# Feed-forward product on the raw stream, with each token's factor put on by GpSimd afterwards

## The chip, the core and the metric

One core of one Trainium2 chip. The metric is the device time of one execution in microseconds (us), the median of several executions. Five engines work side by side, each through its own queue in order, and meet at semaphores: TensorE (PE) multiplies matrices, VectorE (DVE) and GpSimd (POOL) do elementwise work, ScalarE (ACT) copies and applies functions, SyncE (SP) starts transfers.

## The reference, cut to what matters

Two blocks follow each other. The part that the change touches is the feed-forward layer of the first:

```python
h = rmsnorm(x, norm_ffn_g[l])          # x * rsqrt(mean(x*x) + eps) * g, per token
g = dwconv(jnp.einsum("bsd,df->bsf", h, w_gate[l]), conv_ffn_w[l])   # 3 taps over tokens
v = jnp.einsum("bsd,df->bsf", h, w_up[l])
x = x + jnp.einsum("bsf,fd->bsd", jax.nn.silu(g) * v, w_down[l])
```

There are 1024 tokens, 1024 channels, 2816 feed-forward channels. All is float32. The norm's factor `rsqrt(...)` is one number for each token.

## The kernel before

The stream x lies in SBUF as `stream` (`X`), 8 tiles of 128 channels by 1024 tokens. Every product is made of three: a value is split into a high part (rounded by a copy) and a low part (the value minus its high part), for the input (`norm_hi`, `norm_lo`, in code `HH`, `HL`) and for the weights (`w_hi`, `w_lo`), and high*high, low*high and high*low are added in PSUM. Weights come in slabs of 128x1024: SP loads `w_raw` (two buffers), ACT copies the high part (L1078), POOL subtracts for the low part (L429).

The order of the work on each engine is written out by hand; semaphores (`wait_ge`) join the queues. PSUM has 8 banks. Products go round the banks 0 to 3, banks 4 and 5 carry the norm's sums and factors, banks 6 and 7 hold intermediate pieces of the norm and the feed-forward result (`ACC`).

Around the change the program runs like this. The mixer's output product is four "down jobs" of 16 tiles, each tile 6 matmuls for 128 channels by 512 tokens (a half). DVE adds each tile to the stream (`add_out`, L1723), and PE may be four tiles ahead of it, since it writes bank t mod 4 only when the addition that read it is done. During the last down job the feed-forward norm begins: ACT squares each finished stream tile (`square`, L1096), POOL adds the squares up (`sums`, L464, 14 additions into `temp2`), PE sums over channels (`stat`, L644), ACT takes the root (`mean_root`, L1109), DVE the reciprocal (`rstd`, L1534), and PE spreads the factor over a bank (`spread`, L651). The first half's `stat` stands ahead of tile 12 of the down job and its `spread` ahead of tile 13; the second half's stand in the next product, ahead of k=4 and k=5. Numbers m run over 16 pieces: half m // 8, channel tile m % 8.

With the factor there, DVE makes each piece of the normalized stream, x times weight times factor (`scaled`, L1547), ACT copies its high part (`hi`, L1116), and DVE (`low`, L1558) or, for three pieces, POOL (`piece_low`, L448) subtracts. `apply_early` puts the first pieces behind additions 12 to 15, `apply` does the rest. The first feed-forward product, `gated_pair` (L697 to L699), takes the pieces as they are ready.

The feed-forward layer has 22 channel tiles f. Each takes a pair of slabs (gate and up), four product tiles of 24 matmuls. ACT reads a gate tile to `temp0` and an up tile to `temp1` (`ffn_tile`, L1146) in the order gate half 0, up half 0, gate half 1, up half 1, then copies the high parts of two coming weight slabs. DVE applies the three taps to `temp0` after the third read (`ffn_conv`, L1792, L1795, L1798), ACT the silu (L1277), DVE multiplies by `temp1` (L1804), ACT and DVE split the result (L1280, L1808). After each two f a down job of 16 tiles follows on PE, which DVE adds to the stream (`add_down`, L1604), behind the multiplication in DVE's queue. DVE also does six long reductions for the second block's modulation (`ada_products`, L1819) in each turn. A loop runs ten turns; POOL does nothing in it but the low parts of six slabs a turn. The last f has its halves in another order, gate first.

## Time and profile before

| | us |
|---|---|
| median of 3 runs | 2075.82 |
| lowest, highest | 2075.29, 2077.02 |
| the profiled execution, its time | 2077.7 |
| its span in the profile | 2076.0 |
| TensorE busy | 2052.3 (99%) |
| VectorE, ScalarE, GpSimd busy | 1207.4, 669.7, 786.1 |

The span is the time from the first to the last instruction; the execution's own time is 1.7 us more. The granted TensorE clock is 0.996 of full over the execution (2.4 GHz is full). An engine's idle time matters only where another engine waits for it, so the views of waits and of the chain that ended last are read before the busy shares. A matmul's duration in the rows is longer than the distance to the next: matmuls overlap, and the distance is what counts.

### The profile page before, as it was taken

The numbers are of one execution on the slowest core, as the hardware profiler recorded it, in microseconds if no ns is written. First come the engines' busy times: TensorE is split into PE (matmuls) and PEld (weight loads), VectorE is DVE, ScalarE is ACT, GpSimd is POOL, SyncE is SP. The second block draws the span as 40 slices with busy tenths as digits, with TensorE's granted clock in tenths as the row PEclk, the third lists the DMA queues.
The fourth block names the chain that finished last, engine by engine and source line by source line (L and its number), as shares of the span: only waits on it lengthen the run. The fifth ranks groups of instructions, "written<-read, shape, count | busy, mean of one in ns | idle before, by whom it ended". The sixth has DMA issues, their size and how long they took to land.

```text
span 2076.0 us, 24666 instructions
## 1 busy us (share of the span) xinstructions
PE 2052.3 (99%) x9284; PEld 1681.1 (81%) x9284; DVE 1207.4 (58%) x1674; ACT 669.7 (32%) x1147; POOL 786.1 (38%) x471
## 2 busy tenths in 40 slices
PE   9999999999999999999999999999999999999998
PEld 7888788888888888888878888888888878777886
DVE  7999476555644555455566454354464480597565
ACT  6323345221122221222254122122122271698112
POOL 4678826222221222222276132122132272465623
PEclk9999999999999999999999999999999999999998
DMA  4131112322123222232112021121121111010202
GB/s 166 62 112 45 37 51 91 122 101 94 67 110 113 101 73 88 101 121 102 41 39 64 31 71 41 31 71 40 41 61 41 41 42 60 20 43 21 72 11 81
DMA packets 44748, 141.24 MB, mean 68 GB/s; under 512 B 5616, under 2 KB 9856, under 8 KB 44672
## 3 DMA queue, kind: packets, MB, share of 16 engines
q1 hardware_dynamic: 31632, 100.68, 15.1%
q10 hardware_dynamic: 13040, 39.54, 5.1%
q8 instruction: 50, 0.82, 0.2%
q14 instruction: 26, 0.21, 0.0%
HBM read 135.98 MB, written 7.36 MB: 69 GB/s over the span
## 4 chain that ended last, share of the span: by engine, by line
PE 81%; POOL 9%; ACT 5%; DVE 4%; issue 2%; DMA 0%; POOLq 0%; ACTq 0%; SPq 0%; DVEq 0%
PE psum L630 25%; PE psum L632 24%; PE psum L631 24%; POOL temp L464 2%; POOL w_lo L429 2%; POOL temp L489 1%; ACT probs L1470 1%; POOL temp L522 1%; DVE psum L1547 1%; DVE norm_lo L1560 1%; PE psum L972 1%; PE psum L997 1%; PE psum L754 1%; PE psum L756 1%; PE psum L755 1%
## 5 line engine op out<-in xcount | busy, mean ns | idle before, releaser
L429 POOL TENSOR_TENSOR w_lo<-w_raw,w_hi 128x1024 fp32r<-128x1024 f32 x174 | 441.0, 2550 | 975.2 <-ACT w_hi L1078 969.4
L630 PE MATMUL psum<-norm_hi,w_hi 128*128 128x512 f32 x1632 | 636.3, 390 | 1.2 <-ACT temp L1146 1.2
L632 PE MATMUL psum<-norm_hi,w_lo 128*128 128x512 f32 x1632 | 635.0, 389 | 0.0
L631 PE MATMUL psum<-norm_lo,w_hi 128*128 128x512 f32 x1632 | 634.9, 389 | 0.0
L630 PEld LDWEIGHTS psum<-norm_hi,w_hi 128*128 128x128 f32 x1632 | 306.3, 188 | 65.6 <-issue 1.8
L632 PEld LDWEIGHTS psum<-norm_hi,w_lo 128*128 128x128 f32 x1632 | 306.3, 188 | 63.7
L631 PEld LDWEIGHTS psum<-norm_lo,w_hi 128*128 128x128 f32 x1632 | 306.4, 188 | 63.5 <-issue 0.2
L1146 ACT ACTIVATE temp<-psum 128x512 f32<-128x512 f32 x160 | 93.2, 598 | 397.5 <-PE psum L632 371.7
L1606 DVE SCALAR_TENSOR_TENSOR stream<-psum,mods,stream 128x512 f32<-128x512 f32 x160 | 119.7, 750 | 172.1 <-PE psum L632 172.1
L1078 ACT CAST w_hi<-w_raw 128x1024 fp32r<-128x1024 f32 x158 | 159.2, 1046 | 143.0 <-PE psum L632 79.6
L1604 DVE TENSOR_TENSOR stream<-psum,stream 128x512 f32<-128x512 f32 x176 | 118.7, 689 | 83.7 <-PE psum L632 83.5
L1692 DVE SCALAR_TENSOR_TENSOR psum<-glu,vec,psum 128x1024 f32<-128x1024 f32 x116 | 149.6, 1290 | 4.1
L630 PE MATMUL psum<-ffn_y_hi,w_hi 128*128 128x512 f32 x352 | 138.1, 392 | 0.0
L632 PE MATMUL psum<-ffn_y_hi,w_lo 128*128 128x512 f32 x352 | 137.1, 389 | 0.0
L631 PE MATMUL psum<-ffn_y_lo,w_hi 128*128 128x512 f32 x352 | 137.0, 389 | 0.0
L1819 DVE CUSTOM_DVE_ANT_0 ada_raw<-ada_raw,c_act 128x1024 f32<-128x1024 f32 x64 | 117.2, 1889 | 0.0
L1898 DVE TENSOR_TENSOR temp<-temp 128x1024 f32<-128x1024 f32 x40 | 77.4, 1935 | 52.3 <-ACT temp L1146 50.4
L1792 DVE TENSOR_SCALAR psum<-temp,vec 128x1024 f32<-128x1024 f32 x22 | 28.3, 1289 | 134.9 <-ACT temp L1146 134.6
L464 POOL TENSOR_TENSOR temp<-temp 128x512 f32<-128x512 f32 x54 | 70.1, 1298 | 95.4 <-ACT temp L1096 66.6
L630 PE MATMUL psum<-pool_y_hi,w_hi 128*128 128x512 f32 x256 | 99.8, 390 | 0.0
L632 PE MATMUL psum<-pool_y_hi,w_lo 128*128 128x512 f32 x256 | 99.6, 389 | 0.0
L631 PE MATMUL psum<-pool_y_lo,w_hi 128*128 128x512 f32 x256 | 99.6, 389 | 0.0
(218 smaller groups left out, 2968.8 us busy)
## 6 DMA issues: line engine op xcount, KB each, us to landing
w_raw<-in_slabs SPq DMA_DIRECT2D x175, 512.0 KB, 3.5
ada_raw<-in_ada ACTq DMA_DIRECT2D x10, 3072.0 KB, 12.2
stream<-in_x SPq DMA_DIRECT2D x8, 512.0 KB, 9.3
out<-stream SPq DMA_DIRECT2D x8, 512.0 KB, 2.8
skew_scratch<-row_scratch ACTq DMA_DIRECT2D x1, 3072.0 KB, 16.4
ada_raw<-in_ada ACTq DMA_DIRECT2D x1, 2048.0 KB, 7.8
bias<-skew_scratch ACTq DMA_DIRECT2D x4, 512.0 KB, 3.9
c_act<-in_c ACTq DMA_DIRECT2D x1, 512.0 KB, 9.7
```

Of the source, the lines that this page charges most:

```text
L429: nc.gpsimd.tensor_tensor(WL[place][:, :], RAW[at % 2][:, :], WH[place][:, :].bitcast(f32), ALU.subtract).then_inc(slab_ready, 1)
L464: nc.gpsimd.tensor_tensor(dst, squares(n, m - 1) if k == 1 else dst, squares(n, m), ALU.add).then_inc(sum_done, 1)
L630: nc.tensor.matmul(dst, wh, xh, start=n == 0, stop=False)
L631: nc.tensor.matmul(dst, wh, xl, start=False, stop=False)
L632: last = nc.tensor.matmul(dst, wl, xh, start=False, stop=n == len(terms) - 1)
L1078: nc.scalar.copy(WH[place][:, :], RAW[at % 2][:, :]).then_inc(w_hi_done, 1)
L1146: nc.scalar.activation(dst, bank[b], func, scale=scale).then_inc(act_read, 1)
L1604: ins = nc.vector.tensor_tensor(part, src, part, ALU.add)
L1606: ins = nc.vector.scalar_tensor_tensor(part, src, mods[:, gate + e:gate + e + 1], part, ALU.mult, ALU.add)
L1692: step(nc.vector.scalar_tensor_tensor(ACC, window, w, ACC, ALU.mult, ALU.add))
L1819: ins = nc.vector.tensor_tensor_reduce(out=ADA[:, n, :], in0=ADA[:, n, :], in1=c_act[:, :], scale=1.0, scalar=0.0, op0=ALU.mult, op1=ALU.a ...
L1898: step(nc.vector.tensor_tensor(body(T[dst]), body(T[src]), T[src][:, 16 - width:16 - width + S], ALU.add))
```

## The change

The first feed-forward product no longer takes the normalized stream but the stream times the norm's weight, without the token's factor. Each piece is split behind its addition in the last down job: ACT makes the high part in one instruction with the weight as scale, ahead of the square of the same piece, and DVE the low part from the stream, the weight and the high part, behind the next addition. The factor is computed as before; ACT copies it from banks 4 and 5 to `temp2`, where it stays for the whole layer. POOL multiplies it onto each half tile that ACT has read to `temp0` or `temp1`, and DVE's taps and multiplication wait for POOL (`f_scaled`) where they waited for ACT (`act_read`). The three pieces that POOL subtracted for this norm go.

```diff
+            gp.wait_ge(rstd_kept, 4)
+            def ffn_scale(f, order):
+                for n, (T_n, half) in enumerate(order):
+                    gp.wait_ge(act_read, 40 + 4 * f + n + 1)
+                    y = body(T[T_n], half)
+                    nc.gpsimd.tensor_tensor(y, y, body(T[2], half), ALU.mult).then_inc(f_scaled, 1)
+            ffn_scale(0, crossed)
             with gp.Fori(0, FFN_LOOPS) as i:
                 for n in range(FFN_SLAB + 6, FFN_SLAB + 12):
                     lower(n + 6 * i, n, SLAB_PLACE[n])
+                    if n in (FFN_SLAB + 7, FFN_SLAB + 9):
+                        ffn_scale(2 * i + (n - FFN_SLAB - 5) // 2, crossed)
...
-            norm_after_down(FFN, 48, ffn_slabs)
+            for m in range(16):
+                half, k = divmod(m, 8)
+                act.wait_ge(dve_read, 48 + m + 1)
+                nc.scalar.activation(HH[:, k, hs(half)], X[:, k, hs(half)], ACT.Identity, bias=zero[:, :],
+                                     scale=v("ffn_g", k)).then_inc(hi_done, 1)
+                square(FFN, m)
+                if m == STAT_AT[FFN] - 2:
+                    mean_root(FFN, 0)
+            mean_root(FFN, 1)
+            for half in range(2):
+                act.wait_ge(spread_done, spreads(FFN, half))
+                nc.scalar.copy(body(T[2], half), bank[4 + half]).then_inc(rstd_kept, 1)
+            weight_his(32, 34)
...
-            add_out(3, lambda m: apply_early(FFN, m))
-            apply(FFN, 16 - STAT_AT[FFN])
+            def ffn_plain_low(m):
+                half, k = divmod(m, 8)
+                dve.wait_ge(hi_done, m + 1)
+                nc.vector.scalar_tensor_tensor(HL[:, k, hs(half)], X[:, k, hs(half)], v("ffn_g", k),
+                                               HH[:, k, hs(half)].bitcast(f32), ALU.mult, ALU.subtract
+                                               ).then_inc(lo_done, 1)
+            def behind_last(m):
+                if m:
+                    ffn_plain_low(m - 1)
+                if m == STAT_AT[FFN] - 1:
+                    rstd(FFN, 0)
+            add_out(3, behind_last)
+            ffn_plain_low(15)
+            rstd(FFN, 1)
...
-                dve.wait_ge(act_read, a + (2 if last else 3))
+                dve.wait_ge(f_scaled, 4 * f + (2 if last else 3))
...
-                dve.wait_ge(act_read, a + 4)
+                dve.wait_ge(f_scaled, 4 * f + 4)
```

On DVE, at the end of the last down job (additions L1723, reciprocal L1534, the norm's pieces L1547 and L1558), the queue before reads:

```order
L1723 TENSOR_TENSOR stream<-psum,stream 128x512 x25
L1534 RECIPROCAL stat_column<-stat_column 128x4
L1723 TENSOR_TENSOR stream<-psum,stream 128x512
L1547 SCALAR_TENSOR_TENSOR psum<-stream,vec,psum 128x512
L1723 TENSOR_TENSOR stream<-psum,stream 128x512
L1547 SCALAR_TENSOR_TENSOR psum<-stream,vec,psum 128x512
L1558 TENSOR_TENSOR norm_lo<-psum,norm_hi 128x512
```

The same place on DVE after the change (L1738 is the addition, L1801 the new low part, L1549 the reciprocal):

```order
L1738 TENSOR_TENSOR stream<-psum,stream 128x512
L1801 SCALAR_TENSOR_TENSOR norm_lo<-stream,vec,norm_hi 128x512
L1738 TENSOR_TENSOR stream<-psum,stream 128x512
L1801 SCALAR_TENSOR_TENSOR norm_lo<-stream,vec,norm_hi 128x512
L1549 RECIPROCAL stat_column<-stat_column 128x4
L1738 TENSOR_TENSOR stream<-psum,stream 128x512
L1801 SCALAR_TENSOR_TENSOR norm_lo<-stream,vec,norm_hi 128x512
```

Between the additions there was nothing up to the reciprocal; now a low part with both inputs in SBUF stands behind each addition but the first, eleven of them ahead of the reciprocal.

On POOL, the queue from the sums of squares (L463) over the first channel tile to the first half of the loop, after the change (L428 is a slab's low part, L557 the new multiplication):

```order
L463 TENSOR_TENSOR temp<-temp 128x512 x14
L428 TENSOR_TENSOR w_lo<-w_raw,w_hi 128x1024 x4
L557 TENSOR_TENSOR temp<-temp 128x512 x4
L561 UNCONDITIONAL_BRANCH
L561 ISA
L428 TENSOR_TENSOR w_lo<-w_raw,w_hi 128x1024
L427 REGISTER_ALU
L428 TENSOR_TENSOR w_lo<-w_raw,w_hi 128x1024
L555 ISA
L557 TENSOR_TENSOR temp<-temp 128x512
L555 REGISTER_ALU
L557 TENSOR_TENSOR temp<-temp 128x512
```

Each turn of POOL's loop had six slab parts; now it has two, four multiplications, two, four multiplications and two.

## Rows read from the trace of the kernel before

**Rows 1.** The page: the span, and the busy time of each engine.

```profile
span 2076.0 us, 24666 instructions
...
PE 2052.3 (99%) x9284; PEld 1681.1 (81%) x9284; DVE 1207.4 (58%) x1674; ACT 669.7 (32%) x1147; POOL 786.1 (38%) x471
```

**Rows 2.** Waits, 300 to 356 us: waiter, releaser, us in all, times, longest.

```profile
PEld psum L697 <- DVE norm_lo L1558: 1.0, 3, 0.6
PEld psum L651 <- DVE stat_column L1534: 0.6, 1, 0.6
```

**Rows 3.** Waits of PEld (PE's weight loads), whole span.

```profile
PEld psum L630 <- DVE stream L1604: 3.7, 9, 0.4
```

**Rows 4.** Timeline of DVE, 286 to 385 us: start, us, line, what, idle before.

```profile
307.70 0.69 DVE L1723 TENSOR_TENSOR stream<-psum,stream 128x512 f32<-128x512 f32 x1 [1.12 <-PE psum L632]
...
322.21 0.69 DVE L1723 TENSOR_TENSOR stream<-psum,stream 128x512 f32<-128x512 f32 x1 [0.67 <-PE psum L632]
324.40 0.18 DVE L1534 RECIPROCAL stat_column<-stat_column 128x4 f32<-128x4 f32 x1 [1.50 <-ACT stat_column L1109]
324.51 0.69 DVE L1723 TENSOR_TENSOR stream<-psum,stream 128x512 f32<-128x512 f32 x1
```

**Rows 5.** Timeline of POOL, 286 to 385 us.

```profile
312.89 8.49 POOL L464 TENSOR_TENSOR temp<-temp 128x512 f32<-128x512 f32 x6 [0.80 <-ACT temp L1096]
```

**Rows 6.** Timeline of ACT, 286 to 385 us.

```profile
309.56 1.14 ACT L1096 ACTIVATE temp<-stream 128x512 f32<-128x512 f32 x2
```

**Rows 7.** Timeline of PEld, 321 to 336 us.

```profile
321.79 1.08 PEld L644 LDWEIGHTS psum<-ones,temp 128*128 128x128 f32 x8
...
324.63 0.41 PEld L651 LDWEIGHTS psum<-ident,stat_column 128*128 128x128 f32 x4 [0.59 <-DVE stat_column L1534]
...
329.00 0.19 PEld L697 LDWEIGHTS psum<-norm_hi,w_hi 128*128 128x128 f32 x1
```

**Rows 8.** By line, ns: min, median, max of one, and when it ran.

```profile
L1633 DVE SCALAR_TENSOR_TENSOR norm_lo<-stream,vec,norm_hi x16: 742/748/753, 7.8 to 22.5; 128x512 fp32r<-128x512 f32 x16
...
L1158 ACT ACTIVATE norm_hi<-stream,zero,vec x16: 797/802/817, 6.9 to 21.6; 128x512 fp32r<-128x512 f32 x16
...
L1903 DVE SCALAR_TENSOR_TENSOR temp<-temp x16: 1224/1226/3307, 1079.7 to 1572.1; 128x1024 f32<-128x1024 f32 x16
...
L1819 DVE CUSTOM_DVE_ANT_0 ada_raw<-ada_raw,c_act x64: 1214/1215/3406, 361.7 to 999.6; 128x1024 f32<-128x1024 f32 x64
```

**Rows 9.** POOL slab parts beside DVE's two-input operations, and alone: timeline.

```profile
26.38 5.19 POOL L429 TENSOR_TENSOR w_lo<-w_raw,w_hi 128x1024 fp32r<-128x1024 f32 x2 [9.21 <-ACT w_hi L1078]
...
420.83 5.73 POOL L429 TENSOR_TENSOR w_lo<-w_raw,w_hi 128x1024 fp32r<-128x1024 f32 x2 [17.72 <-ACT w_hi L1078]
442.16 4.76 POOL L429 TENSOR_TENSOR w_lo<-w_raw,w_hi 128x1024 fp32r<-128x1024 f32 x2 [15.60 <-ACT w_hi L1078]
```

**Rows 10.** A turn of the feed-forward loop, ACT then DVE: timeline.

```profile
462.31 0.60 ACT L1146 ACTIVATE temp<-psum 128x512 f32<-128x512 f32 x1 [4.84 <-PE psum L632]
462.81 1.99 ACT L1078 CAST w_hi<-w_raw 128x1024 fp32r<-128x1024 f32 x2
464.69 1.02 ACT L1277 ACTIVATE psum<-psum 128x1024 f32<-128x1024 f32 x1
...
460.48 1.29 DVE L1798 SCALAR_TENSOR_TENSOR psum<-temp,vec,psum 128x1024 f32<-128x1024 f32 x1
465.83 1.23 DVE L1804 TENSOR_TENSOR psum<-psum,temp 128x1024 f32<-128x1024 f32 x1 [4.06 <-ACT psum L1277]
466.97 3.12 DVE L1604 TENSOR_TENSOR stream<-psum,stream 128x512 f32<-128x512 f32 x5
```

**Rows 11.** The last channel tile, ACT then DVE: timeline.

```profile
1008.66 0.60 ACT L1146 ACTIVATE temp<-psum 128x512 f32<-128x512 f32 x1 [1.59 <-PE psum L632]
...
1010.03 0.69 DVE L1604 TENSOR_TENSOR stream<-psum,stream 128x512 f32<-128x512 f32 x1
```

**Rows 12.** POOL groups by line: the nearest row to the new multiplication.

```profile
L489 POOL TENSOR_TENSOR temp<-temp,mix_rstd 128x512 f32<-128x512 f32 x36 | 46.3, 1299 | 26.3 <-ACT temp L1146 26.3
```

More of the change, by code:

```diff
@@ L298, in sum_place @@
             return SUM_PLAIN[:, hs(half)] if n == FIN1 else body(T[2], half)
-        POOL_LOWS = [(FFN, m) for m in (9, 11, 13)] + [(POOL, m) for m in (9, 12, 15)]
+        POOL_LOWS = [(POOL, m) for m in (9, 12, 15)]
         POOL_LOWS += [(KV, m) for m in (9, 12, 15)] + [(ATT, m) for m in (1, 4, 10, 13)]
@@ L1113, in hi @@
                 half, k = divmod(m, 8)
-                act.wait_ge(norm_done, APPLIED_BEFORE[n] + m + 1)
+                act.wait_ge(norm_done, APPLIED_BEFORE[n] - APPLIED_BEFORE[POOL] + m + 1)
                 if shift(n, k) is None:
@@ L1254, in _ @@
                 nc.scalar.copy(MYH[j // 2][:, j % 2, hs(half)], c).then_inc(my_hi, 1)
-            def ffn_slabs(m):
-                if m == 15:
-                    weight_his(32, 34)
             weight_his(30, 32)
-            norm_after_down(FFN, 48, ffn_slabs)
+            load_roots()
+            act.wait_ge(squared_gain, 2)
+            nc.scalar.activation(gain_sq[:, :], gain_sq[:, :], ACT.Sqrt).then_inc(rooted_gain, 1)
+            for m in range(16):
[11 more added lines that the diff above has]
+            weight_his(32, 34)
             act.wait_ge(tiles, FFN_TILE)
@@ L1781, in _, with ffn_conv @@
             dve.wait_ge(ln_scaled, 2 * MT)
-            add_out(3, lambda m: apply_early(FFN, m))
-            apply(FFN, 16 - STAT_AT[FFN])
-            def ffn_conv(f, a, first_step, taps, free=True, last=False):
+            def ffn_plain_low(m):
[12 more added lines that the diff above has]
+            rstd(FFN, 1)
+            def ffn_conv(f, first_step, taps, free=True, last=False):
                 if free:
                     dve.wait_ge(f_lo, f)
-                dve.wait_ge(act_read, a + (2 if last else 3))
+                dve.wait_ge(f_scaled, 4 * f + (2 if last else 3))
                 ins = nc.vector.tensor_scalar(ACC, T[0][:, 15:15 + S], taps(0), None, ALU.mult)
@@ L1825, in ada_products @@
                                         vec[:, bass.ds(VEC["ada_b"] + at, count)], ALU.add).then_inc(ada_read, 1)
-            ffn_conv(0, 40, steps[0], ffn_w(0), False)
+            ffn_conv(0, steps[0], ffn_w(0), False)
             ffn_lo(0, 0)
@@ L1859, in _ @@
             dve.wait_ge(gains_done, 4)
-            ffn_conv(FT - 1, 124, steps[0], ffn_w(FT - 1), last=True)
+            ffn_conv(FT - 1, steps[0], ffn_w(FT - 1), last=True)
             steps[0] += 2
@@ L1863, in _ @@
                 y = bank[6 + half]
-                dve.wait_ge(act_read, 126 + half + 1)
+                dve.wait_ge(f_scaled, 4 * FT - 2 + half + 1)
                 nc.vector.tensor_tensor(y, y, body(T[1], half), ALU.mult).then_inc(f_mul, 1)
```

23 lines of the change are left out of this document (7 added, 16 removed).

## The prediction

> **What bounds the kernel now.** I read the busy times first: TensorE is busy for 2052.3 of 2076.0 us [rows 1]. Whatever the change does to the other engines counts only where TensorE comes to wait, or no longer waits. So the second view is TensorE's waits around the norm that is taken apart: 1.0 us in three waits for low parts and 0.6 us in one wait for the token's factor [rows 2]. That is all that stands there to be won. The third is its waits in the whole span: nine of 0.4 us, 3.7 us together, for an addition L1604 [rows 3]. There are nine down jobs in the loop of the feed-forward layer, and the wait is at the fifth tile of each, for the bank of the first. A chain through ScalarE and VectorE ends there just too late in every turn, and a later chain would cost nine times.
>
> **The end of the last down job: more work on VectorE.** Before, VectorE only adds here: 0.69 us of work and 0.67 idle for each tile, so a tile takes TensorE 1.36 us [rows 4]. Now a low part stands behind each addition. Alone it takes 0.75 us [rows 8], and 0.69 + 0.75 = 1.44 is already more than 1.36. More matters that both of its inputs are in SBUF, and that GpSimd adds up the squares at the same time: six sums in 8.49 us, 1.42 each, nearly without a gap [rows 5]. What such operations do to each other is seen elsewhere. A VectorE reduction with two SBUF inputs takes 1.2 us alone and up to 3.4 beside GpSimd; a scalar_tensor_tensor of this kind 1.2 and up to 3.3 [rows 8]. In turn, two slab parts on GpSimd take 4.76 us alone, 5.73 beside 1024-column reductions, and 5.19 beside a 512-column sum [rows 9]. So one waits until the other's instruction is through, and one 512-column VectorE operation sets GpSimd back by 0.43 us. The additions have one input in PSUM and aren't touched: five in 3.12 us beside slab parts is 0.62 each [rows 10]. A turn of one sum and one low part is then 1.30 (a 512-column multiplication on GpSimd is 1.299 [rows 12]) + 0.43 to 0.45 = 1.74 us, against 1.36 for a tile.
>
> The Trainium skill (SBUF — State Buffer, Who interferes with whom) states the same as an exclusive lock on a port pair, held for the whole instruction, for VectorE operations with two SBUF inputs against GpSimd operations that read SBUF. By its letter a turn would be 1.30 + 0.75 = 2.05 us; the trace agrees on the waiting, but shows the smaller 0.43.
>
> **The walk through the queues**, from the times of the profiled run:
> - ScalarE is free at 309.56, where the first square now starts [rows 6]. It makes high part 0 first (0.80 [rows 8]), then square 0 (0.57 apart [rows 6]), high part 1 and square 1, at about 0.7 + 0.57 for a pair, so the first sum starts at 312.2. With six sums from 312.89 and one some 2.1 us ahead of them [rows 5], it started at 310.8 before: 1.4 us later.
> - VectorE adds piece 0 at 307.70 [rows 4], waits for high part 0 (310.4), and has low parts 0 and 1 behind it by 312.4, uncontended. Low part 2 meets the first sum and starts at 313.5. Low part 3 waits for the square and the sum once more (315.5). Then a turn each of 1.74: low part 4 at 317.2, and so on to low part 8 at 324.1. From there the ring addition, high part (0.80), square (0.63), sum (1.30) is as tight as the lock and a turn is about 2.1: low part 10 ends at 328.8.
> - The reciprocal for the first half stands behind low part 10 in VectorE's queue. It comes at 328.9 and not at 324.40 [rows 4]: 4.5 us later. On the way the seventh sum ends at 324.1 and not at 321.38 [rows 5], so TensorE waits ahead of tile 12 already; that wait lies inside the 4.5.
> - TensorE spreads the factor at 329.3 and not at 324.63, and begins the first feed-forward product at 333.7 and not at 329.00 [rows 7]: 4.7 us later. The additions 12 to 15 follow at up to 2.1 us each and don't hold it, since TensorE may be four tiles ahead.
> - In that product the three waits for low parts of 1.0 us [rows 2] go, of which 0.9 was on TensorE's path. The last low part is there at about 337.6, its first use some 9 us later. The second half's sum ends at 338.7, 0.6 us ahead of its use (333.7 + 24 matmuls, four tiles' worth, 5.44 = 339.1). Its factor comes as before, one k later.
>
> Sum: **4.7 - 0.9 = +3.8 us.** Bounds: without any contention the same walk is paced by ScalarE's pairs and gives +0.5; with VectorE's full 0.75 us added to each sum it gives +5.9. I take 0.43 since it is measured on 512 columns.
>
> **The feed-forward loop: four multiplications on GpSimd for each channel tile.** 22 x 4 x 1.30 = 114 us of work on an engine that is busy for 786.1 [rows 1, 12]. What matters is latency in front of the nine waits. The taps start 1.3 to 1.4 us later, behind the third multiplication: the third tap ends at 460.48 + 1.29 + 1.4 = 463.2. But the silu doesn't start before 464.69, since ScalarE first copies two slab parts from 462.81 to 464.80 [rows 10]. The fourth half is read at 462.31 to 462.91, multiplied by 464.3, and used at 465.83 [rows 10]. Both have 1.5 us to spare, so addition and wait stay where they are: 0. That holds because GpSimd's queue has the coming slabs' parts behind the multiplications, as the order of the rows of the change shows. The slab parts themselves come 0.4 us later, for products 20 us off. The six reductions on VectorE meet two more GpSimd operations and end up to 2.4 us later, about when the next taps may start: 0.
>
> **The first and the last channel tile.** After the first, taps and silu are 1.3 to 1.5 us later; TensorE has four banks of 5.44 us ahead: 0. Around the last, the first addition starts at 1010.03, and can move by 1.3 for the multiplication and 1.5 for reductions that met it, to 1012.8 to 1013.5. TensorE needs it at the read at 1008.66 plus four tiles, 1014.1 [rows 11]: 0, at most 0.5. The copy of the factor by ScalarE (twice 0.6) takes the place of sixteen high parts and costs nothing. Transfers depend on the slab parts, which move by less than their cover.
>
> Total +3.8: the profiled execution goes from 2077.7 to 2081.5; the median, which lies 1.9 below that execution, from 2075.82 to **2079.6 us**.
>
> **The rivals.**
> 1. *The lock costs more, or the ring is longer*: 0.6 us and more for each low part as seen by GpSimd, or the whole 0.75. +4.8 to +7, 2081.7 by the full 0.75. For it speaks that the row with 5.19 had one meeting only, and that a semaphore stands between any two sums.
> 2. *The lock hardly bites*, because the low parts fall into gaps between the sums (0.12 us each now, more when ScalarE paces them). +0.5, 2076.3. Against it: gaps shorter than the operation don't hide it.
> 3. *Slower in the loop*: a slab part of 2.4 us gets in front of the third or fourth multiplication, or the multiplication takes longer beside VectorE. From 1.5 us of delay on, each microsecond costs nine; 2.4 us would give 9 x 0.9 = 8, together 2088. Against it speaks the order in GpSimd's queue.
> 4. *Faster*: the 1.0 and 0.6 us of waits go and nothing takes their place, since no piece waits for the factor any more: 2074.5. It would need the reciprocal no later than 324.40, against eleven low parts ahead of it. To be faster by over 0.2% the nine waits of 0.4 would have to go as well, and nothing in the change shortens their chain.
> 5. *The change doesn't do what it says*: the product starts on the raw stream, but nothing waited for the norm to speak of, so freed work on VectorE buys nothing. This holds in all cases above, and by itself gives 2075.8.
>
> **How the numbers follow.** Forecast, with its own spread of +2.8 to +4.8: 0.50. Rival 1: 0.21. Rivals 2 and 5: 0.15. Rival 3: 0.08. Rival 4: 0.06. A measurement of this kernel can tell about 0.2%, 4.2 us, from no change. Of the forecast 0.32 lies under this and 0.18 above. Slower: 0.18 + 0.21 + 0.07 = 0.46. Faster by over 0.2%: 0.04, most of rival 4 if it is so at all. Same: 0.50. The range runs from 2075.4 (under the case without a lock by the spread of the runs) to 2084.5 (past +7, the upper end of rival 1, by the same), and leaves out rival 4 and most of rival 3.
>
> **What the profile of the changed kernel would show.** The reciprocal at 328 to 330, TensorE waiting ahead of both norm steps of the last down job, about 2.4 and 2 us, and the first feed-forward product from about 333.7. Low parts of 1.3 to 1.9 us and not 0.75, and sums 1.74 to 2.1 apart. No waits for low parts in the product. Nine waits of 0.4 in the loop as before, silu still behind the slab copies, POOL busy for about 114 - 4 us more. I am wrong if the low parts take 0.75 beside the sums, or if the nine waits grow.

## The result, and the profile of the changed kernel

| | before | after |
|---|---|---|
| median of 14 runs each, side by side | 2076.79 | 2080.78 |
| lowest, highest | 2073.83, 2079.47 | 2078.75, 2082.37 |
| profiled execution, its span | 2077.7, 2076.0 | 2080.96, 2079.2 |

The changed kernel is slower by 4.0 us: the ratio is 1.002, with a 95% interval from 1.0013 to 1.0027, or 2.7 to 5.6 us. The forecast was +3.8. (Two executions of one kernel below, "six low parts, silu first", took 3453 and 7043 us, far above its nine others, and are left out of its median.)

The page of after, to be read against [rows 1]:

```profile
PE 2053.7 (99%) x9284; PEld 1681.9 (81%) x9284; DVE 1228.4 (59%) x1661; ACT 673.3 (32%) x1149; POOL 912.5 (44%) x556
```

GpSimd is busy for 126 us more and VectorE for 21, and the time moves by four. So it is again TensorE's waits that count. Those of after between 300 and 362 us (waiter, releaser, us in all, times, longest), against [rows 2]:

```profile
PEld psum L653 <- POOL temp L463: 2.4, 1, 2.4
...
PEld psum L660 <- DVE stat_column L1549: 1.1, 1, 1.1
```

The waits for low parts are gone. In their place TensorE waits 2.4 us for the seventh sum (L463 is POOL's sum of squares) and 1.1 us for the reciprocal. In the whole span the nine waits in the loop stand as in [rows 3] (L1619 is the addition that was L1604):

```profile
PEld psum L639 <- DVE stream L1619: 3.7, 9, 0.4
```

VectorE's timeline in the last down job, against [rows 4]: start, duration, line, what, idle time before. L1738 is the addition, L1801 the new low part, L1549 the reciprocal.

```profile
307.53 0.69 DVE L1738 TENSOR_TENSOR stream<-psum,stream 128x512 f32<-128x512 f32 x1 [1.12 <-PE psum L641]
...
311.50 0.74 DVE L1801 SCALAR_TENSOR_TENSOR norm_lo<-stream,vec,norm_hi 128x512 fp32r<-128x512 f32 x1
...
316.54 1.18 DVE L1801 SCALAR_TENSOR_TENSOR norm_lo<-stream,vec,norm_hi 128x512 fp32r<-128x512 f32 x1
317.64 0.68 DVE L1738 TENSOR_TENSOR stream<-psum,stream 128x512 f32<-128x512 f32 x1
318.24 1.20 DVE L1801 SCALAR_TENSOR_TENSOR norm_lo<-stream,vec,norm_hi 128x512 fp32r<-128x512 f32 x1
...
325.04 1.68 DVE L1801 SCALAR_TENSOR_TENSOR norm_lo<-stream,vec,norm_hi 128x512 fp32r<-128x512 f32 x1
...
327.25 1.50 DVE L1801 SCALAR_TENSOR_TENSOR norm_lo<-stream,vec,norm_hi 128x512 fp32r<-128x512 f32 x1
328.68 0.17 DVE L1549 RECIPROCAL stat_column<-stat_column 128x4 f32<-128x4 f32 x1
```

A low part takes 0.74 or 0.75 before the first sum of squares has begun and 1.15 to 1.68 beside the sums; the additions keep their 0.68. In the even stretch, from 316.54 on, it is 1.70 us from one low part to the next. GpSimd's sums in the same stretch, against [rows 5]:

```profile
312.02 1.40 POOL L463 TENSOR_TENSOR temp<-temp 128x512 f32<-128x512 f32 x1 [21.55 <-ACT temp L1105]
314.16 9.81 POOL L463 TENSOR_TENSOR temp<-temp 128x512 f32<-128x512 f32 x6 [0.74 <-ACT temp L1105]
324.89 1.29 POOL L463 TENSOR_TENSOR temp<-temp 128x512 f32<-128x512 f32 x1 [0.92 <-ACT temp L1105]
326.92 1.28 POOL L463 TENSOR_TENSOR temp<-temp 128x512 f32<-128x512 f32 x1 [0.74 <-ACT temp L1105]
```

Six sums take 9.81 us and not 8.49. The two views side by side show how the engines hold each other up. The sum that starts at 324.89 ends at 326.18, and the low part that starts beside it ends at 326.72; the sum that starts at 326.92 ends at 328.20, and its low part at 328.75. The low parts began with 1.14 and 0.95 us of the sum still to come and took 1.68 and 1.50; both end 0.55 us behind the sum. TensorE's weight loads in the same stretch, against [rows 7] (L653 is the first norm step, L660 the spread):

```profile
324.02 1.63 PEld L653 LDWEIGHTS psum<-ones,temp 128*128 128x128 f32 x8 [2.44 <-POOL temp L463]
328.89 0.71 PEld L660 LDWEIGHTS psum<-ident,stat_column 128*128 128x128 f32 x4 [1.11 <-DVE stat_column L1549]
```

The eight loads take 1.63 us and not 1.08, the four 0.71 and not 0.41. The reason stands in the view of stretches: busy TensorE with its count, the granted clock, the DMA share and GB/s.

```profile
320.00:324.00 4.00, 2.00 (x9) 1.00 0.00 0
324.00:326.00 2.00, 1.98 (x9) 0.55 0.00 0
326.00:328.00 2.00, 2.00 (x6) 0.50 0.00 0
328.00:330.00 2.00, 1.61 (x7) 0.50 0.00 0
330.00:332.00 2.00, 2.00 (x9) 0.74 0.00 0
```

After the wait of 2.4 us TensorE's granted clock fell to 0.50, the lower of its two levels (1.2 GHz), until about 331 us. Before, it is 1.00 in all of these stretches.

**Where the 4 us are.** The weight loads of the high parts tell when TensorE is where, in one row for each product: count, duration, first and last start. First of before, between 300 and 1020 us (L697 is the first feed-forward product, L630 all others):

```profile
L630 PEld LDWEIGHTS psum<-norm_hi,w_hi x672: 187/188/188, 352.8 to 1007.5; 128*128 128x128 f32 x168
...
L697 PEld LDWEIGHTS psum<-norm_hi,w_hi x32: 186/188/192, 329.0 to 352.1; 128*128 128x128 f32 x32
```

and of after:

```profile
L639 PEld LDWEIGHTS psum<-norm_hi,w_hi x672: 187/188/188, 357.5 to 1012.2; 128*128 128x128 f32 x168
...
L706 PEld LDWEIGHTS psum<-norm_hi,w_hi x32: 187/188/192, 334.3 to 356.8; 128*128 128x128 f32 x32
```

The first product starts 5.3 us later, the next 4.7 later, and in the whole rest of the layer nothing is added: 654.7 us from the first to the last load in both. The delay is thus complete at 357 us. After the layer it is 4.8 us and stays so. The two spans differ by 3.2 only, since the profiled execution of before had its last column sums of the program at a lower granted clock (0.50 from 2062 to 2068 us; in after it is 1.00 from 2065 to 2067 and 0.86 in the next 2 us). Of before and then of after:

```profile
2060.94 4.47 PEld L1062 LDWEIGHTS psum<-ones,temp 128*128 128x128 f32 x24 [1.64 <-issue]
```

```profile
2065.82 2.85 PEld L1071 LDWEIGHTS psum<-ones,temp 128*128 128x128 f32 x24 [1.67 <-issue]
```

The change doesn't touch this place; it is 1.6 us between single executions, and the medians decide.

In the turn of the loop, against [rows 10], of ACT and then of DVE (L1294 is the silu, L1826 the third tap, L1832 the multiplication):

```profile
466.99 0.60 ACT L1152 ACTIVATE temp<-psum 128x512 f32<-128x512 f32 x1 [4.84 <-PE psum L641]
467.48 1.99 ACT L1087 CAST w_hi<-w_raw 128x1024 fp32r<-128x1024 f32 x2
469.38 1.01 ACT L1294 ACTIVATE psum<-psum 128x1024 f32<-128x1024 f32 x1
```

```profile
466.53 1.29 DVE L1826 SCALAR_TENSOR_TENSOR psum<-temp,vec,psum 128x1024 f32<-128x1024 f32 x1
470.51 1.23 DVE L1832 TENSOR_TENSOR psum<-psum,temp 128x1024 f32<-128x1024 f32 x1 [2.69 <-ACT psum L1294]
471.65 3.12 DVE L1619 TENSOR_TENSOR stream<-psum,stream 128x512 f32<-128x512 f32 x5
```

From the fourth read to the additions it is 4.66 us, as before. The third tap ends 1.37 us later than then, counted from the read, and the silu, which waits for ScalarE's two copies, doesn't see it. The new multiplications over the whole span (min, median, max in ns):

```profile
L557 POOL TENSOR_TENSOR temp<-temp x88: 1283/1302/2275, 351.5 to 1015.1; 128x512 f32<-128x512 f32 x88
```

### The profile page after: what moved, and what is told of

Same layout as the page of the kernel before. It is cut to its first block, busy times and chain, and to the rows that moved or that the text cites. A ratio compares the mean times of both kernels' runs of the same rounds, so it can differ in the third digit from the quotient of the medians.

```text
span 2079.2 us, 24805 instructions
## 1 busy us (share of the span) xinstructions
PE 2053.7 (99%) x9284; PEld 1681.9 (81%) x9284; DVE 1228.4 (59%) x1661; ACT 673.3 (32%) x1149; POOL 912.5 (44%) x556
## 4 chain that ended last, share of the span: by engine, by line
PE 81%; POOL 8%; ACT 5%; DVE 4%; issue 1%; DMA 1%; POOLq 0%; SPq 0%; ACTq 0%; DVEq 0%
PE psum L639 25%; PE psum L641 24%; PE psum L640 24%; POOL w_lo L428 2%; POOL temp L463 2%; POOL temp L488 1%; ACT probs L1485 1%; POOL temp L521 1%; DVE norm_lo L1575 1%; DVE psum L1562 1%; PE psum L981 1%; PE psum L1006 1%; PE psum L763 1%; ACT w_hi L1479 1%; PE psum L765 1%
## 5 line engine op out<-in xcount | busy, mean ns | idle before, releaser
L428 POOL TENSOR_TENSOR w_lo<-w_raw,w_hi 128x1024 fp32r<-128x1024 f32 x174 | 441.0, 2551 | 637.0 <-ACT w_hi L1087 631.3
L557 POOL TENSOR_TENSOR temp<-temp 128x512 f32<-128x512 f32 x88 | 130.3, 1483 | 218.9 <-ACT temp L1152 218.8
L1619 DVE TENSOR_TENSOR stream<-psum,stream 128x512 f32<-128x512 f32 x176 | 118.4, 689 | 81.7 <-PE psum L641 81.5
L1847 DVE CUSTOM_DVE_ANT_0 ada_raw<-ada_raw,c_act 128x1024 f32<-128x1024 f32 x64 | 139.9, 2243 | 0.0
L463 POOL TENSOR_TENSOR temp<-temp 128x512 f32<-128x512 f32 x54 | 72.5, 1342 | 98.0 <-ACT temp L1105 70.8
```

The costliest lines, as they stand in the source:

```text
L428: nc.gpsimd.tensor_tensor(WL[place][:, :], RAW[at % 2][:, :], WH[place][:, :].bitcast(f32), ALU.subtract).then_inc(slab_ready, 1)
L463: nc.gpsimd.tensor_tensor(dst, squares(n, m - 1) if k == 1 else dst, squares(n, m), ALU.add).then_inc(sum_done, 1)
L557: nc.gpsimd.tensor_tensor(y, y, body(T[2], half), ALU.mult).then_inc(f_scaled, 1)
L1619: ins = nc.vector.tensor_tensor(part, src, part, ALU.add)
L1847: ins = nc.vector.tensor_tensor_reduce(out=ADA[:, n, :], in0=ADA[:, n, :], in1=c_act[:, :], scale=1.0, scalar=0.0, op0=ALU.mult, op1=ALU.a ...
```

## The experiments

All times are medians, differences are to the kernel before in the same comparison. A single us is about what 11 runs can tell; where an experiment turns on less, its profile carries the argument. "From piece 0 to the second product" below is the time from the addition of piece 0 in the last down job (307.70 in before) to the first weight load of the second feed-forward product (352.8): 45.1 us in before and 50.0 in after.

| kernel | median | before | difference, 95% |
|---|---|---|---|
| after | 2080.78 | 2076.79 | +4.0 (+2.7 to +5.6) |
| low parts from PSUM | 2077.90 | 2077.31 | +0.6 (-1.7 to +2.1) |
| before, with two-input operations | 2079.93 | 2077.31 | +2.6 (+0.4 to +4.4) |
| no multiplications | 2081.67 | 2077.31 | +4.4 (+2.5 to +6.4) |
| norm's steps in the product | 2080.29 | 2077.31 | +3.0 (+1.2 to +5.0) |
| wait filled | 2080.91 | 2077.28 | +3.6 (+2.7 to +6.4) |
| two more on GpSimd (5 runs) | 2090.72 | 2076.47 | +14.3 (+11 to +17) |
| steps in the product, six low parts | 2076.39 | 2076.47 | -0.1 (-2.1 to +1.7) |
| the same, spread later | 2075.88 | 2077.28 | -1.4 (-2.9 to +0.8) |
| before, silu first | 2073.07 | 2076.47 | -3.4 (-5.2 to -1.5) |
| after, silu first | 2079.18 | 2077.28 | +1.9 (+0.8 to +4.6) |
| six low parts, silu first (9 runs) | 2073.60 | 2076.47 | -2.9 (-5.0 to -1.0) |
| the same, spread later | 2073.45 | 2077.28 | -3.8 (-5.8 to -2.1) |

### Is it the two SBUF inputs of the low parts?

The changed kernel with the low part's first input taken from a PSUM bank; its count and place in the queue stay.

```diff
-                nc.vector.scalar_tensor_tensor(HL[:, k, hs(half)], X[:, k, hs(half)], v("ffn_g", k),
+                nc.vector.scalar_tensor_tensor(HL[:, k, hs(half)], bank[6 + m % 2], v("ffn_g", k),
```

> The changed kernel, but the sixteen low parts take their first input from a PSUM bank and not from the stream; the low parts are wrong numbers for that reason, so this part of the computation is left out. Each VectorE operation keeps its shape and its place in the queue and has one SBUF input in place of two. Theory (VectorE and GpSimd wait for each other): low parts of 0.75 us, sums 1.44 apart, the reciprocal of the first half near 325.5 and not 328.7, no wait of TensorE over 1 us there and so no fall of its clock; +0.5 us against the kernel before. Rival (the work as such, 0.69 + 0.75 against 1.36 for a tile, and high parts on ScalarE): +4, as the changed kernel.

Measured: +0.6, where after has +4.0. Its row of the low parts by line (ns: min, median, max), and that of after:

```profile
L1801 DVE SCALAR_TENSOR_TENSOR norm_lo<-psum,vec,norm_hi x16: 741/746/751, 310.2 to 332.1; 128x512 fp32r<-128x512 f32 x16
```

```profile
L1801 DVE SCALAR_TENSOR_TENSOR norm_lo<-stream,vec,norm_hi x16: 736/1182/1779, 310.2 to 336.3; 128x512 fp32r<-128x512 f32 x16
```

GpSimd's six sums and the reciprocal, of the experiment:

```profile
314.06 8.55 POOL L463 TENSOR_TENSOR temp<-temp 128x512 f32<-128x512 f32 x6 [0.74 <-ACT temp L1105]
```

```profile
325.51 0.18 DVE L1549 RECIPROCAL stat_column<-stat_column 128x4 f32<-128x4 f32 x1 [0.74 <-ACT stat_column L1118]
```

Both engines are back at their times alone, all sixteen low parts at 0.75 us and the sums at 8.55 us for six. The reciprocal comes at 325.51 and not at 328.68, and it now waits for ScalarE, not for VectorE's own queue. So the operations are not too many for VectorE: an addition and a low part together come every 1.26 us in this profile, less than a tile's 1.36. What costs is the source of one input, and with it the sharing with GpSimd. The granted clock stayed at 1.00 between 324 and 336 us. From piece 0 to the second product it is 45.8 us.

The other way round, the kernel before gets the same operations and nothing else of the change. Their results are overwritten later.

```diff
-            add_out(3, lambda m: apply_early(FFN, m))
+            def extra(m):
+                if 1 <= m <= 11:
+                    half, k = divmod(m - 1, 8)
+                    dve.wait_ge(dve_read, 48 + m)
+                    nc.vector.scalar_tensor_tensor(HL[:, k, hs(half)], X[:, k, hs(half)], v("ffn_g", k),
+                                                   HH[:, k, hs(half)].bitcast(f32), ALU.mult, ALU.subtract)
+                apply_early(FFN, m)
+
+            add_out(3, extra)
```

> The kernel before, with one thing added: behind additions 1 to 11 of the last down job VectorE does one 128x512 scalar_tensor_tensor with both inputs in SBUF, into tiles that are written over later. No high parts are moved, the first product waits for the norm as before. Theory: the reciprocal comes at about 328 and not 324.4, the first product 3.5 to 5 us later, +3 to +4.5 us in all. Rival (the loss comes from the product's early start, the high parts on ScalarE or the multiplications on GpSimd): 0 to +1.

Measured: +2.6, a little under the +3 to +4.5 expected. In its profile the addition of piece 0 comes at 308.83 (why, the last section says), and the reciprocal in the same place of the queue, behind the eleventh operation:

```profile
328.91 0.17 DVE L1534 RECIPROCAL stat_column<-stat_column 128x4 f32<-128x4 f32 x1
```

From piece 0 to the reciprocal it is 20.1 us, against 16.7 in the kernel before [rows 4] and 21.15 in after. The eleven operations alone, without a multiplication, another product order or a split, thus make 3.4 of the 4.4 us. The rest, 1.1, fits the high parts that ScalarE makes ahead of the squares: the experiment before this one has them without the sharing, and its reciprocal comes 18.0 us after piece 0, 1.3 later than in before. From piece 0 to the second product it is 48.5 us here, 3.4 more than in before.

### Do the multiplications on GpSimd cost anything?

The changed kernel without them: the factor is left out of the result, and the taps wait for ScalarE's reads as before.

```diff
             def ffn_scale(f, order):
+                return
...
-                dve.wait_ge(f_scaled, 4 * f + (2 if last else 3))
+                dve.wait_ge(act_read, 40 + 4 * f + (2 if last else 3))
...
-                dve.wait_ge(f_scaled, 4 * f + 4)
+                dve.wait_ge(act_read, 40 + 4 * f + 4)
```

> The changed kernel without the 88 multiplications by the token's factor on GpSimd, and the taps wait for ScalarE's reads again; the factor is left out of the result. Theory: the loop costs nothing, so +4 us against the kernel before, as the changed kernel, and the nine waits of 0.4 us stay. Rival (part of the loss is in the loop): 0 to +3.

Measured: +4.4, no less than after, and the nine waits are the same 3.7 us. Eighty-eight operations, 130 us of GpSimd with what they meet, are free.

They are free up to a point, which the prediction put at 1.5 us of delay. Two more of them, with an unused result, ahead of the third in every second channel tile, 2.6 us, go past it:

```diff
+                    for extra in range(2 if more and n == 2 else 0):
+                        nc.gpsimd.tensor_tensor(GYL[:, 1, hs(extra)], y, body(T[2], half), ALU.mult)
                     nc.gpsimd.tensor_tensor(y, y, body(T[2], half), ALU.mult).then_inc(f_scaled, 1)
```

> The changed kernel with two more GpSimd multiplications of 128x512 (1.3 us each, results unused) ahead of the third multiplication of every second channel tile, those that a down job follows: nine in front of one. Theory: the taps have 1.5 us to spare up to the silu and 2.6 are added, so the silu, the multiplication and the first addition come 1.0 to 1.1 later, nine times: +9 to +10 us over the changed kernel, +13 to +14 against the kernel before. Rival (no cover at all): +23 over the changed kernel; rival (GpSimd is off the path altogether): 0 over it.

Measured: +14.3, some 10.3 over after. TensorE's waits in the whole span:

```profile
PEld psum L641 <- DVE stream L1621: 12.8, 9, 1.4
```

The nine waits grow from 0.4 to 1.4 us each, by 9.1 in all, and with them the time from the first load of the second product to the last of the layer, 709.2 us against 700.0 in after. Of 2.6 us of delay 1.0 shows, so 1.6 was covered: the prediction said 1.5, and nine for each us above it.

### Where does the delay enter, at TensorE or at VectorE?

The norm's column sums and spread leave the last down job and stand in the second half of the first product, with the root and the reciprocal behind the rest of their queues. Nothing in that half or the next one needs the factor before the multiplications do.

```diff
                     for k in range(KT):
-                        if half == 0 and norm != ATT:
+                        if norm == FFN:
+                            if half == 1 and k == 0:
+                                stat(FFN, 0)
+                                stat(FFN, 1)
+                            if half == 1 and k == 2:
+                                spread(FFN, 0)
+                                spread(FFN, 1)
+                        elif half == 0 and norm != ATT:
...
-                         norm=FFN if n == 3 else None, between=lambda m, n=n: out_between(n, m))
+                         between=lambda m, n=n: out_between(n, m))
...
-                if m == STAT_AT[FFN] - 1:
-                    rstd(FFN, 0)
...
+            rstd(FFN, 0)
             rstd(FFN, 1)
```

> The changed kernel, with both column sums and both spreads of this norm moved out of the last down job and behind it, to the second half of the first product (k = 8 and 10 of 16), and the reciprocals behind the last low part. TensorE no longer waits for the reciprocal in the down job. Theory: the low parts and sums still hold each other up, and additions come 1.7 to 2 us apart, so TensorE now waits for the bank of addition 13, which is free at about 331: +2.6 us against the kernel before. Rival (only the reciprocal's place behind the low parts costs): -1.4.

Measured: +3.0. The norm's steps no longer hold TensorE, but it now stands at the additions themselves. Its weight loads (the last tiles of the down job, and the first product):

```profile
328.50 0.19 PEld L639 LDWEIGHTS psum<-mix_y_hi,w_hi 128*128 128x128 f32 x1 [0.98 <-DVE stream L1744]
...
332.39 0.19 PEld L713 LDWEIGHTS psum<-norm_hi,w_hi 128*128 128x128 f32 x1 [2.66 <-issue]
```

VectorE's turns of 1.70 us and, late in the job, up to 2.2 hold the tiles of 1.36. The row of the product names no releaser, but its first load comes 0.07 us after the end of addition 13 (332.32), for whose bank the wait was expected. So VectorE's queue is the source, and moving the norm's steps alone only changes who is named.

Then only six low parts stay between the additions, and ten come behind the last:

```diff
-                if m:
+                if 1 <= m <= 6:
                     ffn_plain_low(m - 1)
...
-            ffn_plain_low(15)
+            for m in range(6, 16):
+                ffn_plain_low(m)
             rstd(FFN, 0)
```

> As e4 (column sums, spreads and reciprocals in the second half of the first product), and only the low parts 0 to 5 stand behind additions 1 to 6; additions 7 to 15 follow without one, then low parts 6 to 15. Theory: the additions keep up with TensorE, which waits for nothing there; -1.4 us against the kernel before, 5 less than the changed kernel. Rival (the contention itself costs TensorE time wherever the low parts stand): +1 to +3.

Measured: -0.1. The 4 us of the change are gone, but the 1.4 us below before that I expected aren't there. Its profile has no wait of TensorE up to the product, and then one, behind this on VectorE:

```profile
329.50 15.95 DVE L1807 SCALAR_TENSOR_TENSOR norm_lo<-stream,vec,norm_hi 128x512 fp32r<-128x512 f32 x10
345.37 0.23 DVE L1555 RECIPROCAL stat_column<-stat_column 128x4 f32<-128x4 f32 x2
```

```profile
345.59 0.85 PEld L660 LDWEIGHTS psum<-ident,stat_column 128*128 128x128 f32 x8 [1.72 <-DVE stat_column L1555]
```

Ten low parts take 15.95 us, 1.6 each, beside sums and slab parts, and the reciprocals come behind them; the spread waits 1.7 us, about what was won. If that is all, the spread two k-steps later must give it back:

```diff
-                            if half == 1 and k == 2:
+                            if half == 1 and k == 4:
                                 spread(FFN, 0)
                                 spread(FFN, 1)
```

> The kernel with six early low parts and the norm's steps inside the product's second half, but with the two spreads two k-steps later (before k = 4, not k = 2). In the profile of the kernel it starts from, TensorE waited 1.7 us ahead of the first spread for the two reciprocals, which stand on VectorE behind ten low parts that took 15.95 us. Theory (this wait took back the whole gain): two k-steps are 12 matmuls, 2.7 us, so the wait goes, nothing else is late: 1.7 us below the kernel it starts from, 1.6 us below before, some 2074.8 us. Rival (the missing gain lies elsewhere, the wait was only a symptom): same as before within 0.2%. Rival (the factor now comes too late for the first multiplications and TensorE waits for their tiles): slower than before by 1 us or more.

Measured: -1.4, with the wait gone from the profile:

```profile
345.64 1.02 PEld L660 LDWEIGHTS psum<-ident,stat_column 128*128 128x128 f32 x8
```

The direction and size are as forecast, but the interval takes in zero, so the medians don't show that this version beats the kernel before. The profiles speak for it in this stretch: from piece 0 to the second product it is 44.1 us, against 45.6 in the version it starts from and 45.1 in before.

### What did the fall of the clock cost?

Nine matmuls with an unused result fill the 2.4 us ahead of the first norm step of the changed kernel.

```diff
+                    if norm == FFN and j == STAT_AT[norm]:
+                        for again in range(9):
+                            nc.tensor.matmul(stat_bank(norm, 0), WH[place][:, 0:P], yh[:, 0, hs(half)],
+                                             start=True, stop=True)
```

> The changed kernel, with nine more matmuls of 128 rows by 512 columns (9 x 0.227 = 2.0 us) on TensorE, ahead of the norm's first column sums, into the bank that these overwrite; nothing uses their results. They fill the 2.4 us in which TensorE waited for GpSimd's seventh sum, and cost nothing as long as they end before it. Theory (the long wait is what the fall of the granted clock from 1.00 to 0.5 in the next 7 us followed, and that fall cost 1.0 us): the granted clock stays at 1.00 between 324 and 332 us, the wait ahead of the sums is 0.4 us, the time is 0.5 to 1.0 us below after, some 2080 us. Rival (the fall has another cause, or cost nothing since TensorE waited for the spread anyway): the granted clock falls as before, or the time is that of after.

Measured: +3.6. The granted clock stays at 1.00, though TensorE is idle for longer a little later. Stretches of TensorE (as above), then its weight loads:

```profile
326.00:328.00 2.00, 1.04 (x5) 1.00 0.00 0
328.00:330.00 2.00, 0.67 (x5) 1.00 0.00 0
```

```profile
324.49 0.97 PEld L653 LDWEIGHTS psum<-ones,temp 128*128 128x128 f32 x8 [0.49 <-POOL temp L463]
...
329.33 0.41 PEld L660 LDWEIGHTS psum<-ident,stat_column 128*128 128x128 f32 x4 [2.72 <-DVE stat_column L1553]
```

Most of what the full clock won is waited away ahead of the spread, which comes when the reciprocal does: 1.1 us of wait became 2.7. Behind the spread there is a gain: from GpSimd's first sum (312.02 in after, 312.39 here) to the next product (357.5 and 356.9) it is 1.0 us less. The medians, +3.6 and +4.0, can't confirm a us. So in the profile the fall cost 1.0 of the 4.9 us that after is longer than before from piece 0 to the second product; the 3.9 that stay with the wait filled come with the late reciprocal.

### The nine waits, and whether the multiplications stand in their way

In all kernels ScalarE copies two slab parts ahead of the silu. Turning that round:

```diff
-                if refill:
-                    refill()
                 act.wait_ge(f_conv, f + 1)
                 nc.scalar.activation(ACC, ACC, ACT.Silu).then_inc(f_silu, 1)
+                if refill:
+                    refill()
```

In the kernel before:

> The kernel before with that one edit of e8: silu ahead of the two copies of weight slabs. Theory: the nine waits go, -3.7 us. Rival: 0.

Measured: -3.4, all nine waits gone. In the kernel with six low parts:

> As e5, and in the feed-forward layer ScalarE applies the silu ahead of the two copies of weight slabs and not behind them. Theory: the first addition of each of the nine down jobs comes about 1.1 us earlier, the nine waits of 0.4 us on TensorE go: 3.6 us less than e5, -5 us against the kernel before. Rival (something else ends those waits, or the later copies hold up a slab): as e5 or slower.

Measured: -2.9, where -5 was expected (the next expectation has 2.6 for it, from a median that still held the two long executions). Two causes were open: the multiplications limit the loop once the silu is early, or the 1.4 us missing above are missing here too. Two runs to tell: this kernel with the spread later,

> As e11_e5_spread_later, and ScalarE applies SiLU before it copies the next slab's high parts. Theory (the two edits add up): 3.4 to 3.7 us below e11_e5_spread_later, 5 us below before, some 2071.3 us, and about 1.5 us below the kernel before with only the SiLU edit. Rival (multiplications on GpSimd limit the loop once SiLU is early, as the earlier pair of runs left open with 2.6 us for an edit that gave 3.4 alone): no better than 2073 us.

measured -3.8, which is 2.4 below the kernel without the silu edit where 3.4 to 3.7 was expected; and the changed kernel with this edit alone,

> The changed kernel, with one edit: SiLU before the copies of the next slab. Theory: the nine waits of 0.4 us go as they do in the kernel before, and the loop with multiplications has slack for it: 3.4 us below after, some 2077.2 us. Rival (the multiplications stand in the way of the earlier additions): 2.6 us or less below after.

measured +1.9, so 2.1 less than after's +4.0, where 3.4 was expected. Both medians lie where the rival put them (2073 us or more; 2.6 or less). The profile decides against it all the same. Loads of the high parts as above, of "after, silu first" and of "before, silu first":

```profile
L639 PEld LDWEIGHTS psum<-norm_hi,w_hi x672: 187/188/188, 359.6 to 1011.7; 128*128 128x128 f32 x168
```

```profile
L630 PEld LDWEIGHTS psum<-norm_hi,w_hi x672: 187/188/188, 352.5 to 1004.7; 128*128 128x128 f32 x168
```

That is 652.1 and 652.2 us from first to last, against 654.7 without the edit in both; "the same, spread later" with the edit has 652.1 too. The edit gives 2.6 us in this stretch, with the multiplications or without: they don't stand in its way. The 3.7 us of nine waits, from which I made my expectations, were too much by 1.1: the row counts weight loads, and a matmul loses less than its load waits. In the list of waits of after the matmuls (PE) of the norm's two steps stand with 2.0 and 0.4 us where their loads (PEld) stand with 2.4 and 1.1, and for the nine waits PE has no row at all. The rest of the -3.4 lies outside of the loop. It is no gain of the edit that I can show; some stretches vary by a us between executions (last section).

By the medians no version is shown to beat "before, silu first": with the change repaired in two places and the same edit the kernel has -3.8, it has -3.4, and the intervals overlap. In the profiles the repaired one is about 1 us shorter from piece 0 to the second product (44.1 against 45.0) and equal in the loop. Both are 7 to 8 us faster than the changed kernel.

## Why the prediction was right

**The place and the mechanism** held: nothing of the delay is in the loop, all of it is between 307 and 357 us, and taking away the shared source takes it away. The absolute forecast, 2079.6, was 1.2 under the measured 2080.78, mostly because the kernel before measured 1.0 more in the comparison than in its first three runs. The walk, point by point:

| | before | predicted | after |
|---|---|---|---|
| first sum starts | 310.8 | 312.2 | 312.02 |
| low part 4 starts | | 317.2 | 316.54 |
| low part 8 starts | | 324.1 | 323.37 |
| seventh sum ends | 321.38 | 324.1 | 323.97 |
| low part 10 ends | | 328.8 | 328.75 |
| reciprocal | 324.40 | 328.9 | 328.68 |
| spread | 324.63 | 329.3 | 328.89 |
| first product | 329.00 | 333.7 | 334.3 |
| second half's norm step | | 339.1 | 339.73 |
| next product | 352.8 | 356.6 (+3.8) | 357.5 |

**The turn of 1.74 us** measured 1.70, and that is partly luck, since its two parts were both wrong. I made it of 1.30 for a sum and 0.43 for a meeting. Without low parts a sum takes 1.30 but the next one starts 1.44 after it ([rows 5], six in 8.49): I left the 0.14 between two sums out. And in the turn a sum grows to 1.55, by 0.26 and not by 0.43. The row with 5.19 in [rows 9] misled me: of its 0.43 only 0.25 is the second slab part's own growth; the other 0.18 is a later start, as ScalarE's high part for it ended only at 28.84 us.

By the Trainium skill (SBUF — State Buffer, SBUF: two separate sides) whichever of the two starts first has the shared ports for its whole instruction, and the other waits. I had worked out 2.05 from this and written that the trace shows less. The traces agree with the page; my working was wrong, because an operation that starts beside another waits only for what is left of it. In the eleven profiles of this case that have VectorE operations of this kind beside GpSimd, 127 of them started between 308 and 350 us with 0.37 us or more of a GpSimd operation still to come, from 0.37 up to 2.33. All ended 0.55 us (0.545 to 0.556) after that operation. The other way round, 88 sums started while such an operation ran, and ended 1.12 to 1.18 us after it. So a turn is 0.55 + 1.16 = 1.71. The 0.34 that 2.05 has more are the first 0.20 of a low part and the first 0.14 of a sum, which pass while the other engine still works.

Two smaller slips stand beside this. 0.69 + 0.75 = 1.44 for VectorE alone counts an overlap twice: without the sharing the pair comes every 1.26 us (low parts from PSUM), under the tile's 1.36, so that the work as such was never too much. And 338.7 is 0.4, not 0.6, ahead of 339.1. The table shows a second piece of luck: low part 8 came 0.7 us before the walk, and from there to the end of low part 10 it took 5.4 us and not 4.7, which brought the reciprocal back to the forecast within 0.2.

The bound of "no contention", +0.5, is what the low parts from PSUM measured: +0.6 (-1.7 to +2.1).

**Two errors cancelled in part.** After the spread I left the rest as before: 4.37 us to the first product. It took 5.4, since the granted clock was at 0.50 for part of it. I had weighed TensorE's wait of 2.4 us only by its length, and the prediction has no term for the clock. Against that, the spread came 0.4 us sooner than forecast, and the low-part waits gave back 0.6 and not 0.9 us, as the product's length of 23.8 then and 23.2 now shows. So the term was 4.3 + 1.0 - 0.6 = 4.7 and not 4.7 - 0.9 = 3.8 in the profile, and 4.0 in the medians.

**GpSimd's load** was forecast as 114 - 4 = 110 us more and is 126. The median multiplication is the forecast 1.302, but the mean is 1.483 (130.3 us for 88): I had counted their work without what they meet. It cost nothing, as did the reductions on VectorE, whose median went from 1.215 to 2.301 us; both lie beside slack of TensorE. The addition in the last channel tile starts at 1017.00, 2.3 us later than its shift; 2.8 to 3.5 were allowed, and TensorE doesn't wait.

**Of the rivals**, the first (the lock costs more) asked for 0.6 us or more for each low part as seen by GpSimd; the sums grew by 0.26 each. The second falls with the sums at 9.81 us. The third didn't happen, but its threshold of 1.5 us and its price of nine for each us are real. The fourth needed a reciprocal at 324.40. The fifth, that freed work on VectorE buys nothing by itself, is nearly so: the waits for low parts that went gave 0.6 us.

**What I misjudged in the experiments** is the same kind of thing twice: a step was moved, and what stands ahead of it on its new queue wasn't timed with contention (ten low parts at 1.6 us), and a row of waits of PEld was taken for TensorE's loss.

## What to carry to other kernels

Work that fits into an engine's idle time by its duration alone can still not fit, when its source makes it share with a neighbour whose stream runs without a gap: here operations of 0.75 us between additions became 1.15 to 1.68 each once the sums ran, and made the sums slower too, while the same operations with one input in PSUM fitted in. What a meeting costs is what is left of the other's instruction when yours starts, so ask where in it yours will start. Before moving a step into such a gap, look what stands behind it in the same queue; here it was a 0.17 us reciprocal that TensorE waited for. And once an engine is pacing, moving the waiter only renames the wait: take work out of the pacing queue, then time what comes behind it anew.

## What the runs showed of the hardware that I had not expected

**TensorE's granted clock fell in some of the kernels between 324 and 334 us, and not in others with waits as long.** In after, and in after with the silu first, it fell right behind the wait of 2.4 us. Without multiplications, waits of 2.4 and 2.8 us, it fell at 326; with two more on GpSimd, the same two waits, at 330. In the kernel before with two-input operations, waits of 1.4 and 2.7, and with the wait filled, 0.5 and 2.7, it stayed at 1.00. What decides it these runs don't tell. Another fall stands in all of these profiles, behind a wait of 3.2 us for a sum of the mixer's part, and there the same kernel code gives two sizes. The weight load behind that wait in the kernel before, and the stretches, first of the kernel before and then of the one with six low parts, silu first and spread later, whose work up to there is the same and whose wait is 3.26 us:

```profile
257.28 0.97 PEld L644 LDWEIGHTS psum<-ones,temp 128*128 128x128 f32 x8 [3.23 <-POOL temp L546]
```

```profile
255.00:260.00 5.00, 2.72 (x17) 0.95 0.00 0
260.00:265.00 5.00, 5.00 (x19) 0.71 0.37 105
```

```profile
255.00:260.00 5.00, 2.69 (x13) 0.74 0.00 0
260.00:265.00 5.00, 5.00 (x15) 0.57 0.40 105
```

The two stretches together are at 1.66 and 1.31 of 2. Of the fourteen profiles four are at 1.31 or 1.32 (this one, "before, with two-input operations", "six low parts" and "after, silu first") and ten at 1.66. The four reach the addition of piece 0 in the last down job at 308.83 to 309.58, and nine of the ten at 307.37 to 307.95 (the tenth, "norm's steps in the product", at 308.63, is a us late at that weight load already). So one execution can be over a us longer than another by this alone, a part of the 3.6 and 5.6 us over which the fourteen runs of after and of before spread. Spans of single executions mean little here, and distances from a common point in the same stretch had to carry the comparisons.

**A VectorE operation with two SBUF inputs and a GpSimd operation wait for each other's end, and pay only for what is left of it.** Of a low part of 0.75 us 0.55 come after the sum beside which it started, whether 0.4 or 2.3 us of GpSimd's operation were left; of a sum of 1.30 some 1.16 come after the low part. In the even stretch of after that makes 1.18 and 1.55, and a turn of 1.70. With one input in PSUM neither waits: sixteen low parts of 0.74 to 0.75 and sums of 1.28 to 1.32, side by side.
